# Where the second block's norms make their products: factors in the copy out of the banks, root products mostly on GpSimd, the residual scaled in place

## The reference, cut to what matters

```python
def first_block(x, ...):
    ...
    h = h + swiglu(rmsnorm(h, ffn_norm_g[i]), ffn_w_in[i], ffn_w_out[i])
    return rmsnorm(h, final_norm_g)

def second_block(x, c, ...):
    mod = c_act @ w_mod[l] + b_mod[l]
    sh1, sc1, g1, sh2, sc2, g2 = split(mod, 6)
    h = rmsnorm_2(x, attn_norm_g[l]) * (1.0 + sc1) + sh1
    proj = h @ w_in[l]
    ...
    x = x + g1 * (mix @ w_out[l])
    h = rmsnorm_2(x, mlp_norm_g[l]) * (1.0 + sc2) + sh2
    u = relu(h @ w_ff1[l])
    x = x + g2 * ((u * u) @ w_ff2[l])
    return rmsnorm_2(x, final_norm_g)
```

## Time and profile before

| | us |
|---|---|
| median of 3 runs | 2235.58 (2234.49 to 2241.96) |
| profiled execution | 2238.55 |
| its span, first to last instruction | 2236.6 |

### The profile page before, as it was taken

How to read it: one execution, slowest core, us unless ns; L and a number is a source line. 1 busy time by engine, 2 the same in 40 slices (tenths; PEclk the granted TensorE clock), 3 DMA queues, 4 the chain that set the end, 5 groups by cost and what they waited for, 6 DMA issues and landing times. The chain is left out here.

```text
span 2236.6 us, 29611 instructions
## 1 busy us (share of the span) xinstructions
PE 2162.0 (97%) x11538; PEld 1853.8 (83%) x11538; DVE 1485.7 (66%) x1907; ACT 1037.4 (46%) x1479; POOL 38.3 (2%) x43
## 2 busy tenths in 40 slices
PE   7999999999999999999998899999999999999998
PEld 5888888788888788888887798877888888888887
DVE  5656776588788677788876566556555556556655
ACT  4324555454444334444454556545443344334443
POOL 4000000000000000000000000000000000000000
PEclk9999999999999999999999899998999999999999
DMA  7777433588688797787886424354555555555553
GB/s 266 271 286 269 162 136 112 205 300 310 237 307 306 248 344 299 265 318 282 300 301 224 170 84 148 132 202 156 188 189 188 189 187 188 190 196 187 183 186 132
DMA packets 71049, 494.47 MB, mean 221 GB/s; under 512 B 8091, under 2 KB 8395, under 8 KB 13185
## 3 DMA queue, kind: packets, MB, share of 16 engines
q1 hardware_dynamic: 67968, 480.54, 59.6%
q0 software_dynamic: 2368, 11.32, 1.4%
q10 hardware_dynamic: 576, 0.73, 0.1%
HBM read 490.40 MB, written 2.16 MB: 220 GB/s over the span
## 5 line engine op out<-in xcount | busy, mean ns | idle before, releaser
L1574 DVE TENSOR_TENSOR m_WLO<-m_RAW,m_WHI 128x1024 fp32r<-128x1024 f32 (+2 forms) x712 | 854.7, 1209 | 565.6 <-ACT m_WHI L1256 555.0
L1256 ACT ACTIVATE m_WHI<-m_RAW 128x1024 fp32r<-128x1024 f32 (+2 forms) x712 | 739.0, 1044 | 774.2 <-PE region L898 386.0
L887 PE MATMUL region<-m_HL,m_WHI 128*128 128x512 f32 x1664 | 610.4, 409 | 33.4 <-DVE m_WLO L1574 16.7
L887 PE MATMUL region<-m_H,m_WHI 128*128 128x512 f32 x1408 | 495.7, 397 | 0.0
L888 PE MATMUL region<-m_HL,m_WLO 128*128 128x256 f32 x1664 | 472.5, 284 | 0.0
L887 PEld LDWEIGHTS region<-m_HL,m_WHI 128*128 128x128 f32 x1664 | 319.7, 192 | 113.8 <-issue 37.1
L888 PE MATMUL region<-m_H,m_WLO 128*128 128x256 f32 x1408 | 394.5, 280 | 0.0
L898 PE MATMUL region<-m_WHI,m_HL 128*128 128x512 f32 x1152 | 363.4, 397 | 0.5 <-DVE m_HL L1765 0.5
L888 PEld LDWEIGHTS region<-m_HL,m_WLO 128*128 128x128 f32 x1664 | 321.4, 193 | 0.5
L887 PEld LDWEIGHTS region<-m_H,m_WHI 128*128 128x128 f32 x1408 | 264.1, 188 | 62.0
L888 PEld LDWEIGHTS region<-m_H,m_WLO 128*128 128x128 f32 x1408 | 265.9, 189 | 0.1
(11 more groups left out here) (279 smaller groups left out, 1624.4 us busy)
## 6 DMA issues: line engine op xcount, KB each, us to landing
m_RAW<-in_w_ff SPq DMA_DIRECT2D x128, 1024.0 KB, 4.8
m_RAW<-in_w_mod SPq DMA_DIRECT2D x96, 1024.0 KB, 5.6
m_RAW<-in_ffn_w_in SPq DMA_DIRECT2D x88, 1024.0 KB, 5.6
m_RAW<-in_ffn_w_out SPq DMA_DIRECT2D x44, 1024.0 KB, 6.0
m_RAW<-in_nsa_w_in SPq DMA_DIRECT2D x40, 1024.0 KB, 5.1
m_RAW<-in_nsa_w_out SPq DMA_DIRECT2D x16, 1024.0 KB, 4.8
m_RAW<-in_w_out SPq DMA_DIRECT2D x16, 1024.0 KB, 4.9
m_RAW<-in_w_in SPq DMA_DIRECT2D x10, 1024.0 KB, 5.3
```

The costliest lines, as they stand in the source:

```text
L887: e.matmul(o, wh[:, c:c + 128], both, start=start, stop=fin, skip_group_check=True)
L1256: e.activation(WHI[u % 4][:, 0:(z - a) * ncol], raw[:, a * ncol:z * ncol], ACT.Copy).then_inc(a_hi, 1)
L1574: e.tensor_tensor(WLO[u % 4][:, 0:m], raw[:, a * ncol:z * ncol], WHI[u % 4][:, 0:m].bitcast(F32), ALU.subtract).then_inc(v_lo, 1)
```

## The change

1. **h4, residual in place.** ScalarE's two squares become units of their own: `gainsq` squares X, then VectorE multiplies X by g in place (it waits for that square), then ScalarE squares the product. For the first three quarters the product is put three plan steps behind the add. The transposes read X. The tile `XG` is gone.
2. **Factors.** `G1c` and `G2c` are computed as soon as their part of the modulation is there (unit `factors`), not in `stat`. The copy out of banks 4 and 5 is four activations of 128x256 with the factor as a scale, where it was two of 128x512.
3. **Products with the root.** VectorE makes those of tiles 0, 1 and 2 to 3 as tensor-tensor products (`prod`). GpSimd makes those of tiles 4 to 7, 8 to 11 and 12 to 15, each as one of 128x1024 (`prods`), the second behind the norms of tiles 0 to 3 and the third behind those of tiles 4 to 7, whose buffers they reuse.
4. **Order.** Norms are put four tiles ahead of the matmul step instead of eight.
5. **No `final`.** The add of `out2` scales X by the root in the same instruction.

```diff
@@ make_plan
     def x_ready(s, k):
         x = s["x"]
         if x in normed:
-            while normed[x] < min(KT, k + 9):
-                put("norm", x, normed[x])
+            while normed[x] < min(KT, k + 5):
+                m = normed[x]
+                if m in (0, 1, 2):
+                    put("prod", x, m)
+                if m == 0:
+                    put("prods", x)
+                put("norm", x, m)
                 normed[x] += 1
...
         if s["kind"] == "down1z":
+            put("gainsq", s["arg"], h)
             put("gainhalf", s["arg"], h)
...
-            put("gained", m0)
-            side.extend([None] * 3 + [("xturn", "h4", m0)])
+            put("gainsq", m0)
+            side.extend([None] * 2 + [("gained", m0)] + [None] * 3 + [("xturn", "h4", m0)])
...
-    side.extend(("final", m0) for m0 in range(0, KT, 4))
@@ scalar_program
-                    for b in range(2):
-                        e.activation(XGT[:, m0 + 2 * b:m0 + 2 * b + 2, :], two(bank[4 + b]), ACT.Copy).then_inc(b_out[4 + b], 1)
+                    w.wait_ge(v_gates, 1 if which == "h4" else 2)
+                    g = G1c if which == "h4" else G2c
+                    for i in range(4):
+                        m = m0 + i
+                        ins = e.activation(XGT[:, m, :], two(bank[4 + i // 2])[:, i % 2, :], ACT.Copy, scale=g[:, m:m + 1])
+                        if i % 2:
+                            ins.then_inc(b_out[4 + i // 2], 1)
...
-            elif name == "final":
-                m0, = arg
-                w.wait_ge(v_rstd, 2)
-                for h in range(2):
-                    ins = e.activation(X[:, h, 128 * m0:128 * m0 + 512], XG[:, h, 128 * m0:128 * m0 + 512], ACT.Copy,
-                                       scale=rstdc[:, h:h + 1])
-                ins.then_inc(a_final, 1)
@@ vector_program
-                    e.tensor_tensor(X[:, h, c], GATED[:, h, :], X[:, h, c], ALU.add).then_inc(v_x, 1)
+                    if kind == "out2":
+                        e.scalar_tensor_tensor(X[:, h, c], X[:, h, c], rstdc[:, h:h + 1], GATED[:, h, :], ALU.mult,
+                                               ALU.add).then_inc(v_x, 1)
+                    else:
+                        e.tensor_tensor(X[:, h, c], GATED[:, h, :], X[:, h, c], ALU.add).then_inc(v_x, 1)
...
-                    w.wait_ge(p_part, P.down1z_up)
-                    e.tensor_tensor(XG[:, h, c], X[:, h, c], GROW[:, c], ALU.mult).then_inc(v_gained, 1)
+                    w.wait_ge(a_sumsq, square_no(m0, h, 0))
+                    e.tensor_tensor(X[:, h, c], X[:, h, c], GROW[:, c], ALU.mult).then_inc(v_gained, 1)
...
+            elif name == "prod":
+                x, q = arg
+                a, b = ((0, 1), (1, 2), (2, 4))[q]
...
+                e.tensor_tensor(HT[0][:, a:b, :], XGT[:, a:b, :], by_token(rstd, b - a), ALU.mult).then_inc(v_ht, 1)
             elif name == "norm":
...
-                e.scalar_tensor_tensor(HT[m % 8 // 4][:, m % 4, :], XGT[:, m, :], g[:, m:m + 1], rstd[:, :],
-                                       ALU.mult, ALU.mult).then_inc(v_ht, 1)
-                if m > 0:
-                    low(m - 1)
-                if m == KT - 1:
-                    low(m)
+                base, sh = (0, 0) if x == "h4" else (16, 48)
+                w.wait_ge(p_part, P.ffn1_end if x == "h4" else P.out2_end)
+                product_ready(w, x, m)
+                w.wait_ge(a_norm, base + m + 1)
+                e.scalar_tensor_tensor(LO[:, m, :], HT[m % 8 // 4][:, m % 4, :], mod[:, sh + m:sh + m + 1],
+                                       HI[:, m, :].bitcast(F32), ALU.add, ALU.subtract).then_inc(v_norm, 1)
@@ gpsimd_program
+            elif name == "prods":
+                x, = arg
+                first = 3 if x == "h6" else 0
+                base = 16 if x == "h6" else 0
+                w.wait_ge(b_out[6], filled(("rowcast", 2 if x == "h4" else 3), 6))
...
+                for q in (1, 2, 3):
+                    for b in (4, 5):
+                        w.wait_ge(b_out[b], filled(("xturn", x, 4 * q), b))
+                    if q > 1:
+                        w.wait_ge(a_norm, base + 4 * q - 4)
+                        w.wait_ge(v_norm, base + 4 * q - 4)
+                    e.tensor_tensor(HT[q % 2][:, :, :], XGT[:, 4 * q:4 * q + 4, :], by_token(rstd, 4), ALU.mult).then_inc(o_ht, 1)
```

More of the change, by code:

```diff
@@ L302, in modt @@
             st["acc_busy"] = False
+            if p in (1, 4):
+                put("factors", p // 4)
     def x_ready(s, k):
@@ L982, in rows_turned @@
         def rows_turned(which, m0, halves=(0, 1)):
-            src = XG if which == "h4" else X
             for h in halves:
@@ L1103, in quarter, with product_ready, square_no @@
         return v_x, name_slab("out1" if which == "h3" else "out2", m0)["x0"] + h + 1
+    def product_ready(w, x, m):
+        again = x == "h6"
+        if m < 4:
+            w.wait_ge(v_ht, min(m + 1, 3) + 3 * again)
+        else:
+            w.wait_ge(o_ht, m // 4 + 3 * again)
+    def square_no(m0, h, scaled):
+        return 9 + m0 + (2 * h + scaled if m0 == 12 else 2 * scaled + h)
     def turned_no(which, m0):
@@ L1637, in vector_program @@
                     e.tensor_tensor(mod[:, sl], mod[:, sl], bmod[:, sl], ALU.add).then_inc(v_mod, 1)
+            elif name == "factors":
+                i, = arg
+                w.wait_ge(v_mod, (2, 5)[i])
+                g, c, own = ((G1c, 16, g_att2), (G2c, 64, g_mlp2))[i]
+                e.scalar_tensor_tensor(g[:, :], mod[:, c:c + 16], 1.0, own, ALU.add, ALU.mult).then_inc(v_gates, 1)
             elif name == "makez":
@@ L1797, in vector_program @@
                 r, = arg
[L1798 to L1801, removed]
                 w.wait_ge(a_sumsq, {1: 8, 2: 24, 3: 32}[r])
@@ L1837, in vector_program @@
                 ins.then_inc(v_sinks, 1)
+            elif name == "prod":
+                x, q = arg
+                a, b = ((0, 1), (1, 2), (2, 4))[q]
+                if x == "h4":
+                    w.wait_ge(a_hid, 22)
+                    w.wait_ge(v_hidlo, 22)
+                else:
+                    w.wait_ge(p_values, 32)
+                w.wait_ge(b_out[6], filled(("rowcast", 2 if x == "h4" else 3), 6))
+                w.wait_ge(b_out[4], filled(("xturn", x, 0), 4))
+                w.wait_ge(b_out[5], filled(("xturn", x, 0), 5))
+                e.tensor_tensor(HT[0][:, a:b, :], XGT[:, a:b, :], by_token(rstd, b - a), ALU.mult).then_inc(v_ht, 1)
@@ L1838, in vector_program @@
             elif name == "norm":
                 x, m = arg
[L1840 to L1852, removed]
-                    w.wait_ge(p_part, P.out2_end)
-                    w.wait_ge(p_values, 32)
@@ L1855, in vector_program @@
-                w.wait_ge(b_out[6], filled(("rowcast", 2 if x == "h4" else 3), 6))
-                w.wait_ge(b_out[4 + m % 4 // 2], filled(("xturn", x, m // 4 * 4), 4 + m % 4 // 2))
-                if m >= 8:
-                    w.wait_ge(a_norm, base + m - 7)
-                    w.wait_ge(v_norm, base + m - 7)
-                e.scalar_tensor_tensor(HT[m % 8 // 4][:, m % 4, :], XGT[:, m, :], g[:, m:m + 1], rstd[:, :],
-                                       ALU.mult, ALU.mult).then_inc(v_ht, 1)
@@ L1945, in gpsimd_program @@
                 e.dma_start(biasB[:, :, :], from_table(toep[1], 0, 16)).then_inc(l_biasB, 16)
+            elif name == "prods":
+                x, = arg
+                first = 3 if x == "h6" else 0
+                base = 16 if x == "h6" else 0
+                w.wait_ge(b_out[6], filled(("rowcast", 2 if x == "h4" else 3), 6))
+                if x == "h4":
+                    w.wait_ge(a_hid, 22)
+                    w.wait_ge(v_hidlo, 22)
+                else:
+                    w.wait_ge(p_values, 32)
+                for q in (1, 2, 3):
[5 more added lines that the diff above has]
+                    e.tensor_tensor(HT[q % 2][:, :, :], XGT[:, 4 * q:4 * q + 4, :], by_token(rstd, 4), ALU.mult).then_inc(o_ht, 1)
             elif name == "qrzero":
-                w.wait_ge(v_ht, 16)
+                w.wait_ge(o_ht, 3)
+                w.wait_ge(v_ht, 3)
                 e.dma_start(cosT[:, :], A["c_cos"]).then_inc(l_rope, 16)
```

29 lines of the change are left out of this document (14 added, 15 removed).

## The result

The changed kernel takes 2243.05 us (median of 20 runs, 2238.34 to 2250.29), the kernel before, run beside it, 2234.56 (20 runs). The ratio is 1.0038, with a 95% interval of 1.0028 to 1.0048: slower by some 8.5 us, where I had forecast +2.0. The profiled execution of after took 2241.20 us, with a span of 2239.4.

What follows compares the result with a forecast made beforehand. TensorE, busy 97%, bounds the kernel; only its waits and lower clock can give time back. h4 +1.2 (24.1 - 24.4 + 1.5) and h6 +0.8 (24.1 - 23.3) make +2.0 on the median 2235.58: 2237.6 us, range 2228.5 to 2244.4.

Steps and rivals of the forecast that it cites:

- rival (d): Slower: behind both norms each GpSimd product stands behind one more weight split, 3.4 us a place, 2244.4 us; chance 0.12.
- Part 1, other quarters: First three quarters at h4: the later in-place product costs nothing beside busy TensorE; 0.82 us a quarter if uncovered.
- Part 1, last quarter: At h4 the product waits for the square: some 0.65 us lost at the first half, 0.82 at the second.
- Part 2: Four scaled copies out of the banks instead of two: +0.5 us at each norm; folding the residual's scaling costs nothing.
- hold: GpSimd's two-operand product locks the port shared with VectorE, taken as the full 1.9 to 2.07 us of each product.
- R: Start of the first product with the root at each norm; before the change 1224.68 us at h4, 1506.27 at h6.
- Part 3, exclusion: Products at both norms: GpSimd and VectorE exclude each other on two SBUF operands, so moving products doesn't relieve VectorE.
- The schedule from R: Hand-laid order behind both norms: first matmul 3.0 us after the first product, slab copied out after 24.1.
- +0.65: Extra us at each norm if GpSimd, not VectorE, gets the shared port first at the first product.
- The wait of about 2.9 at tile 8: TensorE waits 2.9 us in each slab for tile 8, which starts 16.0 us after the first product.
- rival (a): TensorE's lower clock returns at one norm or neither: 2.2 or 4.4 us less, 2235.4 or 2233.2; chance 0.23.
- Rival (b): Port lock hardly bites: slabs out 17.8 us after the first product at both norms, 2225.0 us; chance 0.15.

## Why the prediction was off

The side was wrong: I forecast no measurable change (+2.0 us), it is a loss of 8.5. The time lies inside the range, at its upper part, and near rival (d) (2244.4); but (d)'s mechanism is not what made the loss, so that is luck.

- **Part 1, other quarters: the step that failed.** I wrote that splits behind the later wait "have slack against a busy TensorE; cost nothing", and 0.82 a quarter if that cover were missing. I looked at what waits behind the product and not at what the product waits behind. Moving it three plan steps later put two splits and a 2.35 us modulation step in front of it, and TensorE's order puts the transposes in front of its other work. I put these quarters at nothing, and they cost 6.7 us: waits of 2.60 twice and some 1.5 us of lower clock behind the first of them. With the last quarter's 1.3, part 1 was +1.5 in my sum and measures +8.0. Had the product stayed close behind its square, my own price for missing cover would have been about right (0.71, 0.67 and 0.66 against 0.82).
- **Part 1, last quarter: right.** The product starts 0.82 behind the start of the square, the second half's transposes wait 0.83 longer than before; the first half's wait 0.29, not 0.65. In all 1.3 us against 1.5.
- **Part 2: right.** With no hold, the first matmul is at R + 2.50 instead of 1.83 at h4 and at R + 2.56 instead of 2.00 at h6, so 0.67 and 0.56 against my 0.5. The folded scaling of the residual, which I put at nothing, makes each of the eight adds of out2 0.06 us longer (0.746 against 0.685), 0.5 us of VectorE in all.
- **Part 3, exclusion: right in mechanism, product mis-sized.** I took 1.89 to 2.07 us from the squares; it is 2.34 to 2.57, and 3.17 for the third. The square reads one whole tile twice; the product here reads a second tile and repeats its 256 factors for four tiles. A tile times itself is back at 1.89; whether the repeating or the second tile makes the difference was not separated. The Trainium skill (GPSIMD Engine Reference, section 3.1) was nearer: the estimate from it was 2.2 us. No product stood behind a whole split more, so (d) did not happen as priced, three times 1.13 us a place; the third product alone is some 0.7 longer at each place.
- **The schedule from R.** The slab at R + 24.1 was meant for both; it is 25.7 and 24.8. The +0.65 that I priced if GpSimd came first is seen at h4 (first matmul R + 3.89; at h6, where VectorE came first, R + 3.05 as forecast). The wait of about 2.9 at tile 8 is 2.69 and 2.67, and the lower clock returned behind it at both places (granted 0.74 from R + 8 to R + 22), so rival (a) is out for this execution. Behind R the change costs 2.7 by the profiles and I had +0.5, a difference no larger than the scatter of one kernel's slabs; with the copy kept, the same schedule gives no loss in the times.
- **Rival (b)** (no exclusion, slab at R + 17.8, about -5 a place) was near what comes without the hold at h6: 19.0 and 19.1 in the two one-operand runs. At h4 the slab was still out only at R + 23.3. (b) did not happen because the hold is there.
- **Chances.** 0.12 for slower, all on GpSimd's products, was too low because part 1 had no rival of its own.

## What to carry over

When a step is moved later in a plan, list what stands ahead of it on its own engine between the time its data are ready and its new place, and price that sum for whoever waits in order behind it: here 4.8 us of foreign work in front of a 1.3 us product. Moving a two-operand product from VectorE to GpSimd took no load off VectorE here, since VectorE has two-operand work beside it (17.6 to 17.9 us busy in a slab without the move, 18.1 to 19.8 with it); count GpSimd's time as VectorE's. An instruction saved by working in place was worth less here than the overlap that it ended.

## What the runs showed of the hardware

- A GpSimd step of 128x1024 that reads one operand takes 2.85 to 3.05 us, longer than one with two (1.89 to 2.57), but VectorE steps with two operands run inside it at their own 0.42 and 0.48 us. Others beside it were longer (a split 1.51 for 1.22, four low halves 2.44 for 1.66), so it isn't quite free. The Trainium skill (SBUF — State Buffer, Terms) says that the pair of ports shared by the two engines is held for the full instruction and that the loser is fully blocked; the two-operand runs agree, the one-operand runs don't.
- The third GpSimd step at a place, which begins some 0.25 us behind a VectorE split, is 0.7 us longer than the second in every form: 3.17 against 2.48, 2.72 against 1.98 (a tile times itself), 3.59 against 2.85 (one operand). That GpSimd waits for the split there fits this, but was not tried by itself.
- A product of 128x1024 on GpSimd takes 1.89 us where both operands are the same whole tile and 2.34 where the second is another tile, 256 columns repeated four times; on VectorE the latter takes 1.22.
- Released by one event, the two engines can go either way. Started in the same instant (1229.09) GpSimd was served first, and so it was in three more profiles in which it started 0.01 us ahead; VectorE was served first where it was 0.05 us ahead (1509.95).
- A wait of 2.60 us in a stretch where TensorE is otherwise fully busy was followed by the lower clock in one place (1166.37, eight transposes 1.59 us) and not in another (1198.86, 1.07). Two other kernels with the late product show the same: 1.27 and 1.94 us at the second quarter, 1.07 at the third in both.
